# Experts of a mixture layer: token columns stationary, weights moving, two experts alternating in TensorE's column halves

## What is computed

```python
for g in range(N_GROUPS):
    up = jnp.einsum('td,edf->tef', t, w_up[g])        # 1024 -> 512 per expert
    gate, val = jnp.split(up, 2, axis=-1)             # 256 and 256
    hid = jax.nn.silu(gate) * val * comb[:, g, :, None]
    out = out + jnp.einsum('tef,efd->td', hid, w_down[g])   # 256 -> 1024
```

## Time and profile before

| | |
|---|---|
| median of 3 runs | 1833.4 us |
| span of the profiled execution | 1837.7 us |
| TensorE matmul, busy | 1576.0 us (86%), 10102 records |
| TensorE weight load, busy | 1306.9 us (71%) |
| VectorE, busy | 485.0 us (26%) |
| ScalarE, busy | 403.8 us (22%) |
| GpSimd, busy | 128.7 us (7%) |
| moved by DMA | 340.35 MB, mean 185 GB/s over the span |
| mean granted TensorE clock | 0.873 of full speed (2.4 GHz) |

### The profile page before, as it was taken

How to read it: one execution, slowest core, us unless ns; L and a number is a source line. 1 busy time by engine, 2 the same in 40 slices (tenths; PEclk the granted TensorE clock), 3 DMA queues, 4 the chain that set the end, 5 groups by cost and what they waited for, 6 DMA issues and landing times.

```text
span 1837.7 us, 24383 instructions
## 1 busy us (share of the span) xinstructions
PE 1576.0 (86%) x10102; PEld 1306.9 (71%) x10102; DVE 485.0 (26%) x989; ACT 403.8 (22%) x789; POOL 128.7 (7%) x180
## 2 busy tenths in 40 slices
PE   7989986788599999992899899995885899999960
PEld 6889974465588878881799877854564788878850
DVE  2361175444200000004511067125345000000007
ACT  3112122410011122212222246114200121212110
POOL 0200000000000000003300010000000000000013
PEclk9989996797589999996897979897886599999985
DMA  7612126102659999974114220226007299999943
GB/s 291 258 56 100 47 80 210 44 24 99 247 200 357 360 361 346 349 286 172 42 36 142 75 87 1 87 75 187 12 24 289 73 346 361 362 354 345 357 159 106
DMA packets 161797, 340.35 MB, mean 185 GB/s; under 512 B 18610, under 2 KB 53570, under 8 KB 161474
## 3 DMA queue, kind: packets, MB, share of 16 engines
q1 hardware_dynamic: 143698, 274.98, 42.1%
q0 software_dynamic: 13424, 47.65, 7.4%
q10 hardware_dynamic: 4608, 16.78, 2.2%
HBM read 299.57 MB, written 39.81 MB: 185 GB/s over the span
## 4 chain that ended last, share of the span: by engine, by line
PE 81%; DVE 10%; DMA 4%; ACT 3%; issue 1%; POOL 0%; ACTq 0%; SPq 0%; POOLq 0%; DVEq 0%
PE ps L855 27%; PE ps L867 9%; PE ps L665 8%; PE ps L666 8%; PE ps L667 8%; PE ps L835 2%; PE ps L1123 2%; PE ps L915 2%; PE ps L1145 2%; PE ps L786 1%; PE ps L1191 1%; DVE small L1708 1%; DVE x_rows L1716 1%; DMA weight_ring<-in_w_in_a_dram 1%; PE ps L754 1%
## 5 line engine op out<-in xcount | busy, mean ns | idle before, releaser
L855 PEld LDWEIGHTS ps<-work,expert_weights 128*128 128x128 f32 x2048 | 255.9, 210 | 14.7 <-issue 14.7
L855 PE MATMUL ps<-work,expert_weights 128*128 128x64 f32 x2048 | 258.2, 294 | 2.5 <-ACT work L1368 2.5
L855 PEld LDWEIGHTS ps<-work,weight_ring 128*128 128x128 f32 x2048 | 229.9, 192 | 13.0 <-issue 13.0
L855 PE MATMUL ps<-work,weight_ring 128*128 128x64 f32 x2048 | 232.1, 275 | 0.0
L1848 DVE TENSOR_TENSOR work<-ps,work 128x128 f32<-128x128 f32 x64 | 18.7, 292 | 686.3 <-ACT work L1382 686.3
L666 PE MATMUL ps<-weight_ring_r,mix_cols_r 128*128 128x384 f32 (+3 forms) x360 | 121.3, 338 | 0.0
L667 PE MATMUL ps<-mix_cols_r,weight_ring_r 128*128 128x272 f32 x352 | 102.4, 291 | 0.0
L1382 ACT ACTIVATE work<-ps 128x128 f32<-128x128 f32 x64 | 17.8, 278 | 370.3 <-PE ps L855 370.3
L867 PE MATMUL ps<-expert_weights,work 128*64 128x512 f32 x256 | 89.0, 608 | 0.0
L867 PE MATMUL ps<-mix_cols,work 128*64 128x512 f32 x256 | 86.7, 598 | 0.0
L1388 ACT ACTIVATE work<-ps,small 128x512 f32<-128x512 f32 x64 | 40.5, 684 | 144.0 <-PE ps L867 144.0
(11 more groups left out here) (363 smaller groups left out, 2448.4 us busy)
## 6 DMA issues: line engine op xcount, KB each, us to landing
expert_weights<-in_w_up_dram SPq DMA_DIRECT2D x32, 2048.0 KB, 13.9
weight_ring<-in_w_up_dram SPq DMA_DIRECT2D x32, 2048.0 KB, 15.7
expert_weights<-in_w_down_dram SPq DMA_DIRECT2D x32, 1024.0 KB, 15.9
mix_cols<-in_w_down_dram SPq DMA_DIRECT2D x32, 1024.0 KB, 17.4
expert_rows<-work ACTq DMA_DIRECT2D x32, 512.0 KB, 8.6
weight_ring<-in_w_in_a_dram SPq DMA_DIRECT2D x8, 1536.0 KB, 6.5
expert_rows<-expert_weights POOLq DMA_DIRECT2D x16, 512.0 KB, 9.9
weight_ring<-in_w_o_dram SPq DMA_DIRECT2D x4, 2048.0 KB, 12.7
```

The costliest lines, as they stand in the source:

```text
L855: last = mm(bank(j, SLOTS * f, SLOTS * f + SLOTS), WU[b][:, k, P * f:P * f + P], xgT[:, k, SLOTS * j:SLOTS * j + SLOTS], start=(k == 0), s ...
```

## The change

In the up product the operands change places: the 64 token columns of one expert are stationary and a row block of its up matrix (512 columns) moves. The result has slots on the partitions (first expert 0 to 63, second 64 to 127) and the 512 features along the bank. That is 8 matmuls an expert, and the two experts of a pair alternate matmul by matmul, in the two column halves. The banks of the result alternate from pair to pair. The down product alternates in the same way. As the hidden values now come with slots on the partitions, two transposes (`turn_hidden`) and a VectorE copy bring them into the down product's layout. Silu and the product on VectorE run once a pair over 256 elements a partition instead of twice over 128.

The loads are the same in number and size and have the same runs. They are issued by pair: both up matrices once the pair's up product is done (`up_done`), both down matrices once its down product is done. TensorE waits for up and down matrices apart (`up_in`, `dn_in`). The "more" loop is changed alike; its part of the diff is left out here.

```diff
             def experts(l):
 
                 sp.wait_ge(S("wo_mm"), 10 * (l + 1))
-                for b in range(2):
-                    expert(l, b, b)
+                up_weights(l, 0, 0)
+                down_weights(l, 0, 0)
                 sp.wait_ge(S("rt_mm"), NT * (l + 1))
-                for b in range(2, 4):
-                    expert(l, b, b)
+                up_weights(l, 2, 1)
+                down_weights(l, 2, 1)
                 ln_params(2 * l + 1)
                 with sp.Fori(1, NE // 4) as r:
-                    for b in range(4):
-                        sp.wait_ge(S("down_done"), r * 4 + (NE * l + b - 3))
-                        expert(l, r * 4 + b, b)
+                    for q in range(2):
+                        sp.wait_ge(S("up_done"), r * 2 + (PAIRS * l + q - 1))
+                        up_weights(l, r * 4 + 2 * q, q)
+                        sp.wait_ge(S("down_done"), r * 2 + (PAIRS * l + q - 1))
+                        down_weights(l, r * 4 + 2 * q, q)
...
+            def turn_hidden():
+                for f in range(2):
+                    last = tr(bank(6, P * f, P * f + P), h_cols[:, f, :], ident)
                 return last
...
                         pe.wait_ge(S("xgt"), r * 2 + (g + q + 1))
-                        for j in range(2):
-                            b = 2 * q + j
-                            pe.wait_ge(S(f"exp_in{b}"), r * 32 + (16 * s + 32))
-                            for f in range(4):
-                                for k in range(KD):
-                                    last = mm(bank(j, SLOTS * f, SLOTS * f + SLOTS), WU[b][:, k, P * f:P * f + P],
-                                              xgT[:, k, SLOTS * j:SLOTS * j + SLOTS], start=(k == 0),
-                                              stop=(k == KD - 1))
-                            last.then_inc(S("up_done"), 1)
+                        pe.wait_ge(S(f"up_in{q}"), r * 32 + (16 * s + 32))
+                        for k in range(KD):
+                            for j in range(2):
+                                c = slice(SLOTS * j, SLOTS * j + SLOTS)
+                                last = mm(bank(q, rows=(SLOTS * j, SLOTS * j + SLOTS)), xgT[:, k, c],
+                                          WU[2 * q + j][:, k, :], start=(k == 0), stop=(k == KD - 1),
+                                          skip_group_check=True)
+                        last.then_inc(S("up_done"), 1)
                         pe.wait_ge(S("xg_in"), r * 32 + (16 * (g + q) + 32))
                         turn_rows().then_inc(S("xg_free"), 1)
+                        pe.wait_ge(S("h_rows"), r * 2 + (s + q + 1))
+                        turn_hidden().then_inc(S("h_mm"), 1)
+                        pe.wait_ge(S("hid"), r * 2 + (s + q + 1))
                         pe.wait_ge(S("y_ev"), r * 2 + (s + q + 1))
-                        for j in range(2):
-                            b = 2 * q + j
-                            pe.wait_ge(S("hid"), r * 4 + (2 * (s + q) + j + 1))
-                            for half in range(2):
-                                for f in range(2):
-                                    last = mm(bank(4 + half, rows=(SLOTS * j, SLOTS * j + SLOTS)), hid[:, j, f, :],
-                                              WD[b][:, f, 512 * half:512 * half + 512], start=(f == 0),
-                                              stop=(f == 1))
-                            last.then_inc(S("down_done"), 1)
+                        pe.wait_ge(S(f"dn_in{q}"), r * 32 + (16 * s + 32))
+                        for half in range(2):
+                            for f in range(2):
+                                for j in range(2):
+                                    c = slice(SLOTS * j, SLOTS * j + SLOTS)
+                                    last = mm(bank(4 + half, rows=(SLOTS * j, SLOTS * j + SLOTS)), hid[:, f, c],
+                                              WD[2 * q + j][:, f, 512 * half:512 * half + 512], start=(f == 0),
+                                              stop=(f == 1), skip_group_check=True)
+                        last.then_inc(S("down_done"), 1)
...
-                with act.Fori(0, PAIRS) as i:
-                    for j in range(2):
-                        act.wait_ge(S("up_done"), i * 2 + (2 * s + j + 1))
-                        af(sg[:, j, :], bank(j, 0, 2 * SLOTS), ACT.Silu).then_inc(S("gate"), 1)
...
+                with act.Fori(0, PAIRS // 2) as r:
+                    for q in range(2):
+                        act.wait_ge(S("up_done"), r * 2 + (s + q + 1))
+                        af(sg, bank(q, 0, DE), ACT.Silu).then_inc(S("gate"), 1)
...
-                with dve.Fori(0, PAIRS) as i:
-                    for j in range(2):
-                        dve.wait_ge(S("gate"), i * 2 + (2 * s + j + 1))
-                        v.tensor_tensor(hid[:, j].rearrange("p f n -> p (f n)"), bank(j, 2 * SLOTS, 4 * SLOTS),
-                                        sg[:, j, :], ALU.mult).then_inc(S("hid"), 1)
+                with dve.Fori(0, PAIRS // 2) as r:
+                    for q in range(2):
+                        dve.wait_ge(S("gate"), r * 2 + (s + q + 1))
+                        v.tensor_tensor(h_rows, bank(q, DE, 2 * DE), sg, ALU.mult).then_inc(S("h_rows"), 1)
+                        dve.wait_ge(S("h_mm"), r * 2 + (s + q + 1))
+                        v.tensor_copy(hid, bank(6, 0, 2 * P).rearrange("p (f n) -> p f n", f=2)).then_inc(S("hid"), 1)
```

More of the change, by code:

```diff
@@ L300, in build @@
         xgT = view(work, 2 * D, KD, P)
[L301 to L304, removed]
+        sg, h_rows = view(work, 3 * D, DE), view(work, 3 * D + DE, DE)
+        hid = view(work, 3 * D + 2 * DE, 2, P)
+        xg_cols = xg.rearrange("p (k c) -> p k c", k=KD)
+        h_cols = h_rows.rearrange("p (k c) -> p k c", k=2)
         yg = [view(work, 0, 2, D), view(big, 0, 2, D)]
@@ L834, in turn_rows @@
                         kk = 4 * half + k
-                        last = tr(bank(2 + half, P * k, P * k + P), xg[:, kk * P:kk * P + P], ident)
+                        last = tr(bank(2 + half, P * k, P * k + P), xg_cols[:, kk, :], ident)
+                return last
+            def turn_hidden():
+                for f in range(2):
+                    last = tr(bank(6, P * f, P * f + P), h_cols[:, f, :], ident)
                 return last
@@ L876, in experts @@
                     with pe.Fori(0, more) as x:
-                        pe.wait_ge(S(f"more_step{l}"), x * 9 + 2)
-                        pe.wait_ge(S(f"more_x{l}"), x * 16 + 16)
+                        pe.wait_ge(S(f"more_step{l}"), x * 11 + 2)
+                        pe.wait_ge(S(f"more_x{l}"), x * 32 + 16)
                         turn_rows().then_inc(S(f"more_step{l}"), 1)
-                        pe.wait_ge(S(f"more_step{l}"), x * 9 + 4)
+                        pe.wait_ge(S(f"more_step{l}"), x * 11 + 4)
                         pe.wait_ge(S(f"more_w{l}"), x * 32 + 32)
-                        for f in range(4):
-                            for k in range(KD):
-                                last = mm(bank(0, P * f, P * f + P), WU[0][:, k, P * f:P * f + P], xgT[:, k, :],
-                                          start=(k == 0), stop=(k == KD - 1))
+                        for k in range(KD):
+                            last = mm(bank(0), xgT[:, k, :], WU[0][:, k, :], start=(k == 0), stop=(k == KD - 1))
                         last.then_inc(S(f"more_step{l}"), 1)
-                        pe.wait_ge(S(f"more_step{l}"), x * 9 + 7)
+                        pe.wait_ge(S(f"more_step{l}"), x * 11 + 7)
+                        turn_hidden().then_inc(S(f"more_step{l}"), 1)
+                        pe.wait_ge(S(f"more_step{l}"), x * 11 + 9)
                         for half in range(2):
                             for f in range(2):
-                                last = mm(bank(4 + half), hidx[:, f, :], WD[0][:, f, 512 * half:512 * half + 512],
+                                last = mm(bank(4 + half), hid[:, f, :], WD[0][:, f, 512 * half:512 * half + 512],
                                           start=(f == 0), stop=(f == 1))
```

79 lines of the change are left out of this document (42 added, 37 removed).

## The result

The changed kernel takes 1691.1 us (median of 4 runs, 1687.7 to 1698.5) against 1836.1 us before (1829.9 to 1841.8): a ratio of 0.921, 95% interval 0.918 to 0.925, 145 us less. The forecast was 1698. The span of the profiled execution is 1688.4 us, 149.3 less than before.

A forecast was written before the change was run, and what follows sets the result against it. TensorE was taken to set the pace at 20.66 us a pair, then weights at 18.2. Stages of 277.9 us (10 + 1.5 + 254.8 + 2.5 + 9.1) take 135.8 off the 1837.7 span; less 4.3, 1698 us, range 1678 to 1770.

The forecast's parts named there:

- What bounds: Expert stages: TensorE sets the pace before at 20.66 us a pair; after, the weights' transfers do.
- Up product 6.9 us, down 3.4: TensorE's products per pair: alternating column halves overlap fully, halving serial time, from 14.5 us up and 5.4 us down.
- The overlap read from the seam of two experts: Old down product: 16 records take 5.42 us instead of 6.9, so records of different halves run side by side.
- Chain 2.4 us: Between up and down product: Silu, product, two transposes, copy and hand-overs take 2.4 us, against about 1 us before.
- 18.2 us a pair: Weight transfers after the change: 7.3 MB at 411 GB/s take 17.8 us, plus 0.4 for the gather.
- the 0.4 us that I added for the gather: Allowance in each pair's transfer time for the gather, in whose window the rate was 374 GB/s.
- The transfers don't stop: Weight queue: with a whole pair still queued while TensorE waits, it doesn't drain, so the rate holds 411 GB/s.
- The rival with 0.27: Transfers keep today's mean of 353 GB/s, 20.7 us a pair, only 32.9 us a layer gained: 1768 us; chance 0.27.
- Clock: TensorE waits some 5 us a pair; a half-speed start costs 2 us, 14.8 us a pair, hidden under 18.2.
- Early release: Issuing loads sooner: 25 us a layer of the gain, before the loads start.
- The sum: One layer's expert stage: 277.9 us instead of 345.8, 67.9 less a layer, 135.8 for two.

The follow-up runs named there:

- e8: Kernel before with long runs (16 KB a partition) for its up matrices alone, token columns turned to match: 1835.1 us, ratio 0.999.
- e1: Kernel before with the change's load part alone (weights issued by pair, up matrices released after the up product): 1833.7 us, ratio 1.0005.
- e5: Changed kernel, loading in the loop only the first of eight depth blocks of each up matrix: 1547.5 us, ratio 0.844.
- e4: Changed kernel with weights laid out in runs of 16 KB (up) and 8 KB (down), the same bytes: 1667.3 us, ratio 0.908.
- e9: Changed kernel without column halves in the up product, each matmul over the whole array into a bank of its own: 1795.2 us, ratio 0.979.
- e2: Changed kernel with up and down matrices of a pair both issued only once its down product is done: 1692.8 us, ratio 0.923.
- e6: Changed kernel with up matrices of a pair issued only after the next pair's up product, so the queue drains: 1948.5 us, ratio 1.062.
- e7: Kernel before with only the down product's two experts alternating matmul by matmul in the two column halves: 1778.0 us, ratio 0.967.
- e10: Kernel before, gathering in the loop only 16 of 128 token rows for each pair: 1842.6 us in one run.
- e12: Kernel before with each pair's result rows issued by SyncE behind the weight transfers instead of by ScalarE: 1835.5 us in one run.
- e3: Changed kernel without alternation: in both products all matmuls of the first expert precede those of the second, still in different halves: 1717.2 us, ratio 0.936.

## Why the prediction was right

- **What bounds.** Right on both sides: e8 and e1 show that neither quicker nor earlier transfers were worth anything before, e5 and e4 that the transfers are the bound after.
- **Up product 6.9 us, down 3.4.** 7.0 to 7.1 and 3.65 (the last record's latency counted). The overlap read from the seam of two experts held for the whole product. e9 gives the price without it, 14.0 for my 13.8.
- **Chain 2.4 us.** It is 1.97 (509.12 to 511.09 in the first stage, 627.42 to 629.38 above); the hand-overs cost less than I gave them. TensorE's pair is 12.4 us for my 12.8.
- **18.2 us a pair.** 17.8: from the up product at 533.30 to that at 746.67 are 12 pairs. The rate is 414 for my 411, and of the 0.4 us that I added for the gather hardly any is there: at 414 GB/s the 7.3 MB of a pair, gathered rows included, take 17.6 to 17.7 us.
- **The transfers don't stop.** The step on which most hung. The rival with 0.27, that they keep to 353 GB/s over a stage, is refuted by the 414. The ceiling of about 358 GB/s on the page "DMA: Bandwidth & Descriptors" of the Trainium skill, section Specifications, doesn't hold for this core, which works alone: 414 over 200 us, and 429 over 160 us with long runs.
- **Clock.** As forecast it falls to half in the waits for weights: up products that begin so take 8.4 to 9.8 us instead of 7.1 (from 605.43, 8.47; from 746.67, 9.52). It hides behind the transfers, except in the last pair of a stage, behind which no weights are left to wait for: there the 2.4 us of the row from 746.67 are paid.
- **Early release.** I gave it as 25 us a layer of the gain. That was the one misattribution. Counted from the start of the first stage the loads do start 24 us earlier (496.97 - 487.24 = 9.7 against 524.16 - 489.99 = 34.2). But 18 of these are the first up product, 9.5 us instead of 27.6: fewer records, side by side, and a clock that rises on the way (granted 0.74 over 487.3 to 496.7, against 0.50 over 490 to 519 before). With the late release of e2 the loads still start at 14.9, so the release itself moves them by 5.2 us, of which 3.6 reach the end of the first stage; in the second, as told above, nothing does.
- **The sum.** 277.9 us a stage forecast, 274.5 measured. The weights take about 253 us from first to last byte (498 to 751) for my 257.3, the start before them is 0.7 us shorter, and the tail is 10.7 for my 9.1, since the last up product begins at half clock. Against the span the forecast was 13.5 us too long (1701.9 against 1688.4): 6.8 in the two stages, 6.7 in parts that the edit doesn't touch. That the median came within 7 us of 1698 is partly luck: the profiled span lay 4.3 us above the median of the runs that I had before, and it lies 2.7 below the median after.

## What to carry to other kernels

Two fp32 matmuls in different column halves ran fully side by side when their order alternated, and partly when it did not; here one such pair in the trace before, and the step between weight loads, were enough to work out the gain of the rest. When an engine with no gap stands beside transfers at 0.97, look at the rate in short windows: here it was lost in the stretches after each restart, and a faster consumer kept the queue full and so raised the rate from 353 to 414 GB/s by itself. Test who sets the pace with an edit that quickens one side alone, and repeat it after each change: long runs were worth 0 before and 24 us after.

## What the runs showed of the hardware that I had not expected

- A run's size still counted above 2 KB: 414 GB/s with runs of 2 and 4 KB, 429 with 8 and 16 KB, over 160 us.
- From 1 to 7 us after a train was issued to a queue that had run out or nearly so, transfers ran at 231 to 382 GB/s (before, e1, e6, e7, e8, e10 and e12), lowest in the kernel before (231 to 265). In e6 and e1 they stayed below 400 until 14 us after the issue. The cause is open.
- Records of one product overlapped with those of the next where they lay in different column halves (e3) (L883 and L868 in turn from 593.39 on). The order of the instructions was no barrier between the halves there.
